# First norm's modulation and first projection by quarters of the features, with idle turns ahead and later loads in another order

## The reference, cut to what matters

```python
cond = silu(c)                                        # c: one row of 1024
mod  = cond @ ada_w[0] + ada_b[0]                     # 1024 -> 6144
sh1, sc1, g1, sh2, sc2, g2 = split(mod, 6)            # 1024 each
h = rms_norm(x, ln1_g) * (1 + sc1) + sh1              # first norm, x: 256 x 1024
z = h @ w_in[0]                                       # 1024 -> 2840, float32
# z: queries, compressed/selected/window keys and values, gates, MoBA q, k, v
# head norms, compressed branch (nsa_cmp_w1, nsa_cmp_w2), attention, w_out
x = x + g1 * mixer;  h2 = rms_norm(x, ln2_g) * (1 + sc2) + sh2
x = x + g2 * sparse_moe(h2)                           # 32 experts, top 4
# then the second model: 2 layers (attention, RG-LRU) with squared-relu MLPs
```

## Time and profile before

| what | us |
|---|---|
| median of 3 runs (lowest, highest) | 1799.84 (1799.42, 1801.1) |
| the profiled execution: its time | 1800.52 |
| its span, first to last instruction | 1798.3 |
| PE busy in the span | 1727.9 (96%) |
| first product of the first projection | starts at 23.41 |
| fourth column piece (v = 6) | starts at 66.02 |
| hidden layer of the compressed branch | starts at 104.34 |
| first turn of the attention's weights | starts at 129.62 |

### The profile page before, as it was taken

One profiled execution on the slowest core, in us unless ns is written; L12 is line 12 of the kernel. 1 busy time (PEld: TensorE's weight loads), 2 busy tenths in 40 slices (PEclk: granted clock), 3 DMA queues, 4 the chain that ended last, 5 costly groups with the idle time before them and its releaser, 6 DMA issues.

```text
span 1798.3 us, 24508 instructions
## 1 busy us (share of the span) xinstructions
PE 1727.9 (96%) x9927; PEld 1053.3 (59%) x9928; DVE 657.9 (37%) x1231; ACT 262.4 (15%) x529; POOL 130.1 (7%) x188
## 2 busy tenths in 40 slices
PE   7999999999999998999989999999999999999998
PEld 4457533333333333333333333787899998899987
DVE  2655412122112121221212212214578545768743
ACT  1145211011011010101101011204111001511100
POOL 4116300000000001001010010100100000010000
PEclk9999999999999999999999999999999999999999
DMA  8988999969999999999999999631244443535440
GB/s 321 357 278 277 388 415 428 428 277 429 428 429 427 429 427 429 427 428 428 429 428 429 428 428 422 238 141 47 94 169 159 158 171 118 199 141 187 156 173 24
DMA packets 95504, 548.07 MB, mean 305 GB/s; under 512 B 6002, under 2 KB 9282, under 8 KB 68722
## 3 DMA queue, kind: packets, MB, share of 16 engines
q1 hardware_dynamic: 95298, 546.93, 75.6%
q10 hardware_dynamic: 144, 0.26, 0.0%
HBM read 546.12 MB, written 1.05 MB: 304 GB/s over the span
## 4 chain that ended last, share of the span: by engine, by line
PE 75%; DMA 21%; SPq 1%; ACT 1%; DVE 1%; issue 1%; DVEq 0%; ACTq 0%
DMA ring<-in_exp_w 20%; PE ps L1294 17%; PE ps L1515 11%; PE ps L1325 8%; PE ps L1352 7%; PE ps L1544 6%; PE ps L1585 5%; PE ps L953 2%; PE ps L1259 2%; PE ps L1246 2%; PE ps L1383 2%; PE ps L1167 2%; PE ps L1614 2%; PE ps L926 1%; PE ps L1639 1%; PE ps L1410 1%
## 5 line engine op out<-in xcount | busy, mean ns | idle before, releaser
L1294 PE MATMUL ps<-ring,sq 128*64 128x512 f32 x2112 | 464.6, 593 | 25.1 <-DMA ring<-in_exp_w 25.1
L1294 PEld LDWEIGHTS ps<-ring,sq 128*64 128x64 f32 x2112 | 146.8, 137 | 318.1 <-issue 263.7
L1325 PE MATMUL ps<-arena,sq 128*64 128x512 f32 x1056 | 233.9, 595 | 3.4
L1325 PEld LDWEIGHTS ps<-arena,sq 128*64 128x64 f32 x1056 | 75.3, 137 | 140.8 <-issue 140.5
L2249 DVE TENSOR_SCALAR sq<-arena,rstd 128x64 f32<-128x64 f32 x68 | 19.5, 329 | 365.2 <-PE ps L1294 364.5
L2322 DVE TENSOR_SCALAR hn<-ps 128x512 f32<-128x512 f32 x33 | 22.8, 692 | 319.9 <-PE ps L1294 319.9
L1766 ACT ACTIVATE sq<-hn 128x512 f32<-128x512 f32 x33 | 20.8, 629 | 529.2 <-DVE hn L2322 529.2
L1659 ACT ACTIVATE sq<-ps 128x512 f32<-128x512 f32 (+1 forms) x99 | 51.9, 524 | 308.6 <-PE ps L1325 212.2
L1515 PE MATMUL ps<-arena 128*128 128x136 f32 (+1 forms) x768 | 90.0, 277 | 0.0
L1352 PE MATMUL ps<-hn,ring 128*128 128x272 f32 x384 | 88.8, 393 | 0.0
L1515 PEld LDWEIGHTS ps<-arena 128*128 128x128 f32 x768 | 88.6, 191 | 0.0
(11 more groups left out here) (410 smaller groups left out, 2099.3 us busy)
## 6 DMA issues: line engine op xcount, KB each, us to landing
ring<-in_exp_w SPq DMA_DIRECT2D x123, 2048.0 KB, 21.1
arena<-in_exp_w SPq DMA_DIRECT2D x68, 2048.0 KB, 19.6
ring<-in_mlp_w_up SPq DMA_DIRECT2D x16, 2048.0 KB, 7.4
ring<-in_mlp_w_down SPq DMA_DIRECT2D x16, 2048.0 KB, 7.8
ring<-in_ada_w SPq DMA_DIRECT2D x8, 2048.0 KB, 12.3
ring<-in_sb_w_qkv SPq DMA_DIRECT2D x6, 2048.0 KB, 14.3
ring<-in_w_in SPq DMA_DIRECT2D x5, 2048.0 KB, 12.3
ring<-in_ada_w SPq DMA_DIRECT2D x8, 1024.0 KB, 9.8
```

The source lines that it names most:

```text
L1294: last = mm(bank(2 + part)[64 * h:64 * h + 64, :], lhs, w[:, k % 2, at:at + 512], start=False, stop=(k == C - 1))
L1325: last = mm(bank(3)[64 * h:64 * h + 64, :], m.aT[:, q, 64 * half:64 * half + 64], w[:, q, 512 * h:512 * h + 512], start=(half == 0 and q = ...
```

## The change

1. **Modulation by quarters.** The four parts of `mod` are quarters of the outputs (128 of each 512, for sh1 and sc1) over all 1024 inputs, instead of half by half. Each part is 64 instructions of 128 columns. Copy, turn, bias, scale and the norm's products follow by quarters, two feature chunks each.
2. **First projection by quarters.** w_in's first 1304 columns (pieces 0 to 2, v = 0 to 5) come in four loads `inq` of 256 input rows each. PE goes through v = 0 to 3, then the next quarter of the modulation, v = 4, the turn, v = 5, and on to the next quarter. Banks: `z_bank` puts v = 4 into bank 4 and v = 5 into bank 7. The later pieces stay whole.
3. **The start.** PE runs 3 idle products of `ident` with itself before it waits for c, and 20 before it waits for the tokens. DVE copies the turned tokens, ACT only squares them and loads the table of Sqrt ahead of that. The parameters of set 0 are turned before the first modulation.
4. **Loads.** The order is as below; set 1 of the small parameters is issued after load 4 (it was 3). Slots are freed by other signals: `cmp` by the end of v = 9 (`z_done` 10, of `in 4`), where it was freed by the third `add_modulation`.
5. **Group 1.** DVE adds three quarters, now after head norms 2, 3 and 4; the fourth is done by PE within `modulation_sum`, which stands after the compressed branch's second layer. Its turn follows ahead of the compressed keys' turn, and the first two `modulation_half` of group 2 stand behind the compressed scores.

```diff
+QUARTERS = 4
+IN_FIRST = 1304
+A_LOADS = ([(kind, 0, q) for q in range(QUARTERS) for kind in ("mod", "inq")]
+           + [("in", 0, 3), ("ada", 1, 0), ("in", 0, 4), ("ada", 1, 1), ("ada", 1, 2), ("in", 0, 5), ("cmp", 0, 0),
+              ("ada", 1, 3)] + [("ada", 2, k) for k in range(4)] + [("wout", 0, h) for h in range(2)])
...
-    if (kind, c) == ("in", 0):
-        return "in_first", 1
+    if kind == "inq":
+        return ("in_first", c + 1) if c < QUARTERS - 1 else ("z_done", 6)
     if (kind, layer) == ("ada", 1):
-        return "mod_added", c + 1
+        return ("mod_added", c + 1) if c < 3 else ("mod_parts", 8)
...
+    def idle_turns(count):
+
+        for _ in range(count):
+            mm(bank(6)[:, 0:P], ident, ident, start=True, stop=True)
+
+    idle_turns(3)
     pe.wait_ge(s["c_loaded"], 16)
     turn_params(bank(0), 0, C)
+    idle_turns(20)
     pe.wait_ge(s["x_loaded"], 16)
...
+    def first_modulation(q):
+
+        w = a_slot(A_LOADS.index(("mod", 0, q))).rearrange("p (n k f) -> p n k f", n=2, f=256)
+        for k in range(C):
             for r in range(4):
+                last = mm(bank(MOD_BANK[0])[32 * r:32 * r + 32, P * q:P * q + P], m.condR[:, k, :],
+                          w[:, r // 2, k, P * (r % 2):P * (r % 2) + P], start=(k == 0), stop=(k == C - 1))
...
     def modulation_sum(group):
 
-        pe.wait_ge(s["mod_added"], 4)
+        w = a_slot(A_LOADS.index(("ada", group, 3))).rearrange("p (k n) -> p k n", n=2048)
+        for kk in range(2):
+            for r in range(4):
+                mm(bank(MOD_BANK[group])[32 * r:32 * r + 32, :], m.condR[:, 6 + kk, :], w[:, kk, 512 * r:512 * r + 512],
+                   start=(kk == 0), stop=False)
+        pe.wait_ge(s["mod_added"], 3)
...
+    def project_quarter(v, q):
+
+        c, t = v // 2, v % 2
+        c0, w = IN_CHUNKS[c]
+        wt = a_slot(A_LOADS.index(("inq", 0, q)))[:, 0:2 * IN_FIRST].rearrange("p (k n) -> p k n", n=IN_FIRST)
+        for kk in range(2):
+            k = 2 * q + kk
             if v == 0:
+                pe.wait_ge(s["h_ready"], k + 1)
+            last = mm(bank(z_bank(v))[:, 0:w], m.hn[:, k, META + P * t:META + P * t + P], wt[:, kk, c0:c0 + w],
+                      start=(k == 0), stop=(k == C - 1))
...
+    for q in range(QUARTERS - 1):
+        for v in range(4):
+            project_quarter(v, q)
+        first_modulation(q + 1)
+        project_quarter(4, q)
+        turn_first_modulation(q + 1)
+        project_quarter(5, q).then_inc(s["in_first"], 1)
+    for v in range(6):
+        project_quarter(v, QUARTERS - 1).then_inc(s["z_done"], 1)
         if v == 1:
-            pe.wait_ge(s["root_ready"], 1)
             turn_meta()
...
         elif v == 9:
-            modulation_sum(1)
             pe.wait_ge(s["turned_dve"], 2)
             turned_pairs(5, 0, 2)
         elif v == 10:
-            turn_modulation(1)
...
     last.then_inc(s["cmp_kv_done"], 1)
+    modulation_sum(1)
     pe.wait_ge(s["turned_act"], 2)
     turned_pairs(4, Z_QM, 2)
...
     turned_pairs(0, Z_KM, 2)
-    modulation_half(2, 0)
-    modulation_half(2, 1)
+    turn_modulation(1)
     pe.wait_ge(s["cmp_dve"], CMP_DVE.index("k_ready") + 1)
...
     last.then_inc(s["cmp_scored"], 1)
+    modulation_half(2, 0)
+    modulation_half(2, 1)
...
-        for part in {0: (0, 1), 2: (2,)}.get(c, ()):
-            add_modulation(part)
-        if c == 3:
+        if c == 2:
+            add_modulation(0)
+        elif c == 3:
             blocks(0, 4, 0)
             blocks(1, 5, 1)
-            add_modulation(3)
-            modulation_rows(1)
+            add_modulation(1)
         elif c == 4:
...
-            modulation(1)
+            add_modulation(2)
...
     v.tensor_reduce(m.cstat[0:64, 0:1], m.hid2[0:64, 0:64], AX.X, ALU.add).then_inc(s["cmp_dve"], 1)
+    modulation_rows(1)
     dve.wait_ge(s["turned"], 8)
...
     v.tensor_copy(m.kcn[0:64, 0, :], m.kcn[0:64, 1, :]).then_inc(s["cmp_dve"], 1)
+    modulation(1)
```

More of the change, by code:

```diff
@@ L496, in source @@
         if kind == "mod":
[L497 to L502, removed]
+            src = a["ada_w"][0].rearrange("(k p) n -> p k n", p=P)
+            at = 256 * c
+            return [(slice(0, P), 2048, 256, src[:, :, at + D * n:at + D * n + 256]) for n in range(2)]
+        if kind == "inq":
+            src = a["w_in"][0, 256 * c:256 * c + 256, 0:IN_FIRST]
+            return [(slice(0, P), 2 * IN_FIRST, IN_FIRST, src.rearrange("(k p) n -> p k n", p=P))]
         if kind == "in":
@@ L853, in sum_squares, with turn_first_modulation @@
         last.then_inc(s["norm_summed"], 1)
[L855 to L859, removed]
+    def first_modulation(q):
+        w = a_slot(A_LOADS.index(("mod", 0, q))).rearrange("p (n k f) -> p n k f", n=2, f=256)
+        for k in range(C):
             for r in range(4):
-                last = mm(bank(MOD_BANK[0])[32 * r:32 * r + 32, 256 * h:256 * h + 256], m.condR[:, 4 * rows + k, :],
-                          w[:, r // 2, k, 256 * (r % 2):256 * (r % 2) + 256],
-                          start=(rows == 0 and k == 0), stop=(rows == 1 and k == 3))
+                last = mm(bank(MOD_BANK[0])[32 * r:32 * r + 32, P * q:P * q + P], m.condR[:, k, :],
+                          w[:, r // 2, k, P * (r % 2):P * (r % 2) + P], start=(k == 0), stop=(k == C - 1))
         last.then_inc(s["mod_parts"], 1)
[L866 to L871, removed]
+    def turn_first_modulation(q):
+        pe.wait_ge(s["mod_rows"], q + 1)
+        turn(bank(MOD_TURN_BANK[0])[:, P * q:P * q + P], m.modrow[:, P * q:P * q + P], ident).then_inc(s["mod_turned"], 1)
     def modulation_half(group, half):
@@ L988, in compressed_hidden @@
         last.then_inc(s["cmp_hidden"], 1)
-    for v in range(4, 12):
+    for v in range(6, 12):
         pe.wait_ge(s["z_copied"], v - 3)
@@ L2003, in first_modulation @@
         v.tensor_tensor(dst, src, bias, ALU.add).then_inc(s["mod_ready"], 1)
-        dve.wait_ge(s["mod_ready"], h + 1)
-        half = slice(4 * h, 4 * h + 4)
-        link(v.scalar_tensor_tensor(m.affine[:, half], m.modT[:, M_SC1 + 4 * h:M_SC1 + 4 * h + 4], 1.0,
-                                    col(PC_LN1 + 4 * h, 4), ALU.add, ALU.mult))
-        for c in range(4 * h, 4 * h + 4):
+        dve.wait_ge(s["mod_ready"], q + 1)
+        link(v.scalar_tensor_tensor(m.affine[:, pair], m.modT[:, M_SC1 + 2 * q:M_SC1 + 2 * q + 2], 1.0,
+                                    col(PC_LN1 + 2 * q, 2), ALU.add, ALU.mult))
@@ L2017, in program_vector @@
+    for b in range(4):
+        dve.wait_ge(s["x_turned"], b + 1)
+        v.tensor_copy(m.xT[:, 2 * b:2 * b + 2, META:TT], bank(1 + b).rearrange("p (c t) -> p c t", c=2)).then_inc(
+            s["x_placed"], 1)
+    dve.wait_ge(s["prm_turned"], 2)
+    v.tensor_copy(m.prm[:, C:PARAM_ROWS[0]], bank(0)[:, 256 + C:256 + PARAM_ROWS[0]]).then_inc(s["prm_ready"], 1)
     dve.wait_ge(s["x_placed"], 4)
```

97 lines of the change are left out of this document (36 added, 61 removed).

## The result

| | us |
|---|---|
| before, median of 6 runs beside it (lowest, highest) | 1800.05 (1799.37, 1801.1) |
| after, median of 6 runs (lowest, highest) | 1807.24 (1805.62, 1807.73) |
| ratio, 95% interval | 1.0038 [1.0027, 1.0048] |
| the profiled execution of after: time, span | 1805.9, 1804.1 |

The kernel became slower by 7.2 us, where 1.8 was forecast. It is outside the range, and beyond the 0.2% that a measurement tells.

What follows compares the result with a forecast made beforehand. PE was taken to pace the program, so a shift at the attention's end would pass one to one. -3.7 - 2.05 + 3.5 + 2.0 + 1.85 + 0.2 = +1.8 on 1799.84 gave 1801.6 us, range 1796.0 to 1806.5.

Steps and rivals of the forecast that it cites:

- Start of the projection, -3.7: First projection on PE: starts at 19.7 instead of 23.41 us, through idle products and DVE copies beside ACT squares; -3.7 us.
- The mix that the prediction solved for: Sum of squares before the change: some 9 of 16 instructions ran slowly, so the clock rose after about 3.9 us of work.
- The last rival: At the start: clock not up by 9 us, idle products only delay token turns; -1.0 instead of -3.7, 1804.3 us; chance 0.06.
- Gaps, -2.05: PE's waits of 0.42 us for a modulation part and 1.63 us for a w_in piece both go; -2.05 us.
- Modulation parts, +3.5: Within the projection: three new parts at 2.4 us replace two old at 1.86; +3.5 us (+1.9 to +7.4).
- the choice of 2.4: Time in us assumed for one new modulation part, between 1.86 by columns and 3.7 by pairs of weight load and product.
- The load of nsa_cmp_w1, stall +2.0: Ahead of the compressed hidden layer: 8.0 us from signal to needed landing, load takes 10; PE stalls +2.0 us (0 to 9.8).
- full rate: Skill's 512 B at line rate, 429 GB/s: compressed load lands 7.8 us after the signal, stall 0; rival 1799.6 us, chance 0.08.
- Group 1, +1.85 and +0.2: PE gains the fourth quarter's 16 instructions, +1.85 us; waits around the compressed keys add +0.2 us (-0.5 to +1.5).
- Later loads: `ada 2 1` waits for v = 11's end, `ada 2 2` lands 12 us behind, needed 13.7 behind; no cost.
- "Slower": Outcome that the kernel becomes measurably slower, by more than about 0.2% (3.6 us); chance 0.28.
- that of the compressed load: Rival before the hidden layer: biases and `in 5` delay the landing, stall 8 instead of 2; +7.8, 1807.6 us; chance 0.14.

Runs made afterwards that it cites:

- f1: Kernel after with idle products at the first quarter's turn, ahead of the hidden layer and at the compressed keys; 1802.42 us, ratio 1.0012.
- g1: Kernel after without the 3 and 20 idle products ahead of c and of the tokens; 1804.04 us, ratio 1.0028.
- f4: f3 without the 3 and 20 idle products ahead of c and of the tokens; 1796.96 us, ratio 0.9987.
- g2: f4 without its idle products at the first quarter's turn and at the compressed keys; 1800.68 us, ratio 1.0001.
- g3: f4 without the products of Group 1's fourth quarter; 1781.6 us, not comparable because tokens go to other experts.
- f3: f2 with idle products around the first quarter's turn and ahead of the compressed keys; 1799.51 us, ratio 0.9997.
- e2: Kernel after with 3 idle products ahead of each of the two waits at the compressed keys; 1805.16 us, ratio 1.0025.
- e3: Kernel after with `ada 1 1` loaded ahead of `in 4` and added by DVE earlier, freeing the compressed load's slot sooner; 1805.93 us, ratio 1.003.
- e4: Kernel before with only the start of the change; halves, loads and Group 1 as before; 1800.74 us, ratio 0.9999.
- e1: Kernel after with 10 idle products in the wait ahead of the compressed branch's hidden layer; 1803.75 us, ratio 1.0016.
- f2: e3 with the expert biases' loads issued behind nsa_cmp_w1; 1801.46 us, ratio 1.0012.

## Why the prediction was wrong

**The step that failed** is the one that the sum did not have. The prediction read from the rows that PE ran at two levels (3.67 us for the 16 token turns, 5.79 for the sum of squares) and used it for the idle products, in the direction of a gain. It then let PE wait longer in three places (1.69 and 0.99 us around the turn of the first quarter, 2.53 for the compressed load, 0.54 and 0.64 at the keys), priced each wait by its length alone, and did not ask what PE's pace would be behind it. Each fall cost 1.5 to 1.7 us on top of the wait, 4.8 in all, and with the waits filled these were gone (f1). That the rows of before show no fall was no comfort: from 23.41 to 130 us its largest waits were 1.63 and 0.59 us, and none stood close to another. At the start it had two close together, the 0.62 of the line below and the 1.22 of the earlier trace rows, in sum 1.84 us against the 2.68 of after:

```profile
21.75 0.44 PE L870 MATMUL ps<-ident,arena 128*128 128x128 f32 x2 [0.62 <-DVE arena L1998]
```

Whether the sum or the closeness decides is not shown; g1 had 1.50 and 1.27 there without a fall.

**Start of the projection, -3.7: measured -2.92,** the clock up as said. The missing 0.8 us lie in the sum of squares: forecast to end at 14.7, just behind the last square, it began at 11.82 and took 3.69, to 15.5, though the last square was done at 13.5; PE's own time set its end. (The mix that the prediction solved for is also off by its own numbers: (5.79 - 3.4) / 0.215 is 11 of 16 slow instructions and not 9, which would move the end of the idle products from 9.5 to 9.8.) What the forecast had wrong beyond this is that the idle products help at all: they end at 9.7, where the tokens are there at 6.3, and without them the start is at 19.0 to 19.4 (f4, g1, g2, g3). The gain at the start comes from the rest of the change there. The last rival (*Idle turns don't do what they say*) had this direction right, though not its reason, a clock that is not up.

**Gaps, -2.05: right,** both are gone. **Modulation parts, +3.5: measured +1.9,** 1.88 us each (27.54 to 29.42 in f1), the lower bound. For this shape time went by columns: 64 instructions of 128, 29 ns each, where 32 of 256 took 58 ns each. The rule of the Trainium skill that the prediction weighed ("TensorE: Matmul & The Clock Gate", "LDWEIGHTS (loading the stationary operand)") gave 27 ns as an estimate for a weight load, and with it the floor; the trace agrees, and the choice of 2.4 was too dear. Against that stands a term that I had at nothing: from the start to v = 6 a kernel without falls (f3, 20.49 to 63.90) takes 43.41 us where the two terms give 42.61 - 2.05 + 1.95 = 42.51. A quarter (30.57 to 41.80) takes 0.4 us more than its instructions at their durations of before; which of the shorter runs of products loses it was not tried.

**The load of nsa_cmp_w1, stall +2.0: measured +2.53,** its landing 10.1 us behind the issue against 10. The estimate made with the 290 GB/s of the row came out. By full rate (the Trainium skill, "DMA: Bandwidth & Descriptors", "Specifications", at 512 B) the load would have landed 7.8 us behind, as an estimate, and about in time; the trace disagrees again. Small in itself, this wait drew a fall right behind it.

**Group 1, +1.85 and +0.2.** The stretch to flip 0 was forecast at +3.6 and measured at +5.08, of which 1.6 is the third fall: 3.5 without it. **Later loads** cost nothing, as said; but a shift does not go through the experts one to one, 1.2 us came back.

**Chances and range.** Of the rivals none described this. "Slower" had 0.28, spread over mechanisms of which only that of the compressed load was partly at work. The sum with the falls is 1801.6 + 4.8 = 1806.4; the range ended at 1806.5 and the median is 1807.24. These last 0.8 us are not traced.

## What to carry to other kernels

When an edit opens or lengthens a wait in an engine that had run with few pauses, price the stretch behind the wait too, at both levels of the clock. The waits that had a fall behind them here were between 1.2 us (0.54 and 0.64 together) and 3.33 us, and not in every execution. To find such a loss, compare the duration of the same group of instructions before and after, and the granted clock in windows of a few us; the span's mean to three digits tells of it only roughly. First take away the cause of the wait. Where the wait must stay, fill it: at the keys 12 idle instructions left the time from the last turn ahead to `modulation_half` at 4.02 us against 4.00 (e2). Idle products ahead of work that is ready hold that work back: here the token turns by 3.4 us, and the median by 2.55 (f3 to f4).

## What the hardware showed that I had not expected

- The granted clock was at 0.57 to 0.59 in stretches of 4 us behind PE waits of 1.69 and 0.99, 2.53, and 0.54 and 0.64 us, at a cost of 1.5 to 1.7 us each; behind 1.86 us it did not fall in e3's profiled run. In e4, behind 3.33 us, it was 0.50 for 4 us and more, and 16 products took 9.91 us instead of 7.11.
- It is not the same in each execution: e3's runs are at 1801.4 and 1802.6, or at 1805.7 and above; g2's spread over 6.7 us. With the waits filled they spread over 1.4 and 1.5 us in f3 and f4, and over 2.5 in f1.
- The keys' waits of 0.54 and 0.64 us, unchanged in six profiled runs, had a fall behind them in after, g1 and g2 and none in e1, e3 and f2. What else decides stays open.
- The mean granted clock of a run goes with its time in the changed kernels: in g2 0.999 for 1796.8 to 1797.7 us, 0.996 for 1803.5. In the kernel before it tells only the worst ones (0.996, all above 1802.5); else it is a poor guide: a span of 1797.1 had 0.997, and one of 1797.9 had 1.0.
- The same load took 10.1, 17.8, 18.6 and 19.1 us from issue to landing in after, before, e3 and f2. From the start of v = 6 to the landing it was 39.2 us in after, 38.6 in e3, where the issue came 10 us earlier, and 34.6 in f2, where it stood ahead of the biases as well: with full engines, the earlier issue behind the same loads moved the landing little, and going ahead of the biases moved it by 4 us.
